# Scan matrices read back as rows from DRAM, and another order of the state-space items: a two-layer hybrid trunk on one core

## The reference, cut to what matters

```
dt = exp(log_dt);  a = exp(lambda * dt)              # complex, one per group g and state p
b_bar = ((a - 1) / lambda) * b                       # 64 groups, 64 states, 16 inputs
x[l,g,p] = sum_h u[l,g,h] * b_bar[g,p,h]
h[l] = a * h[l-1] + x[l]                             # over 256 tokens
y = Re(sum_p c[g,h,p] * h[l,g,p]) + d * u            # then gelu, a GLU gate, silu(z)
```

## Time and profile before

| what | value |
|---|---|
| median of 3 runs | 952.5 us (952.48 to 952.61) |
| the profiled execution | 952.75 us, of it 951.0 us span |
| PE busy | 936.0 us, 98% of the span |
| DVE busy | 610.0 us, 64% |
| ACT busy | 575.4 us, 60% |
| POOL busy | 111.3 us, 12% |
| chain that ended last | PE 82%, ACT 7%, DVE 6%, issue 3% |
| HBM | 173 GB/s over the span |

### The profile page before, as it was taken

The page is one execution under the profiler, slowest core; times in us unless marked ns, Lnnn a source line. Parts: engine busy times, 40 slices in busy tenths (PEclk is TensorE's granted clock), DMA queues, the critical chain, the costliest instruction groups (busy, mean ns, idle before and its releaser), DMA issues.

```text
span 951.0 us, 15769 instructions
## 1 busy us (share of the span) xinstructions
PE 936.0 (98%) x5939; PEld 796.3 (84%) x5939; DVE 610.0 (64%) x971; ACT 575.4 (60%) x928; POOL 111.3 (12%) x126
## 2 busy tenths in 40 slices
PE   7999999999999999999999999999999999999998
PEld 7998888778878999888888788888888888888886
DVE  4688889799797954855644555555555555555553
ACT  4689886876967746544545573555456545554332
POOL 3101002011020000000002540220021002200000
PEclk9999999999999999999999999999999999999999
DMA  8776544445343467555999986668999866654662
GB/s 285 185 190 196 156 133 134 136 135 175 112 140 127 137 198 266 179 192 190 175 166 180 195 239 169 182 174 160 171 160 172 197 175 178 176 175 156 212 213 85
DMA packets 116007, 165.83 MB, mean 174 GB/s; under 512 B 19301, under 2 KB 56298, under 8 KB 115690
## 3 DMA queue, kind: packets, MB, share of 16 engines
q1 hardware_dynamic: 99504, 159.67, 64.0%
q10 hardware_dynamic: 16442, 5.33, 2.3%
HBM read 162.86 MB, written 2.11 MB: 173 GB/s over the span
## 4 chain that ended last, share of the span: by engine, by line
PE 82%; ACT 7%; DVE 6%; issue 3%; DMA 1%; POOL 1%; ACTq 0%; SPq 0%; DVEq 0%
PE bank L456 21%; PE bank L458 21%; PE bank L457 21%; PE bank L483 3%; PE bank L484 3%; PE bank L485 3%; ACT wh L969 2%; ACT res L1078 2%; PE bank L600 1%; ACT res L1090 1%; DVE wl L977 1%; ACT scr L1230 1%; DVE scr L1747 1%; PE bank L592 1%; DMA res<-in_x 1%
## 5 line engine op out<-in xcount | busy, mean ns | idle before, releaser
L977 DVE TENSOR_TENSOR wl<-raw,wh 128x1024 fp32r<-128x1024 f32 x295 | 362.0, 1231 | 252.7 <-ACT wh L969 251.5
L969 ACT ACTIVATE wh<-raw 128x1024 fp32r<-128x1024 f32 x295 | 310.5, 1058 | 190.2 <-PE bank L458 119.5
L456 PE MATMUL bank<-wh,xh 128*128 128x512 f32 x768 | 307.1, 400 | 0.3 <-DVE wl L977 0.3
L458 PE MATMUL bank<-wh,xl 128*128 128x512 f32 x768 | 300.0, 391 | 0.0
L457 PE MATMUL bank<-wl,xh 128*128 128x512 f32 x768 | 299.2, 390 | 0.0
L458 PEld LDWEIGHTS bank<-wh,xl 128*128 128x128 f32 x768 | 144.1, 188 | 31.1
L456 PEld LDWEIGHTS bank<-wh,xh 128*128 128x128 f32 x768 | 144.3, 188 | 29.0 <-DVE wl L977 0.7
L457 PEld LDWEIGHTS bank<-wl,xh 128*128 128x128 f32 x768 | 144.5, 188 | 27.7
L456 PE MATMUL bank<-wh,yh 128*128 128x512 f32 x256 | 100.5, 393 | 0.0
L458 PE MATMUL bank<-wh,yl 128*128 128x512 f32 x256 | 99.7, 390 | 0.0
L457 PE MATMUL bank<-wl,yh 128*128 128x512 f32 x256 | 99.6, 389 | 0.0
(11 more groups left out here) (317 smaller groups left out, 1022.4 us busy)
## 6 DMA issues: line engine op xcount, KB each, us to landing
raw<-in_o_w_in SPq DMA_DIRECT2D x128, 512.0 KB
raw<-in_e_w_in SPq DMA_DIRECT2D x130, 256.0 KB, 3.3
raw<-in_e_w_out SPq DMA_DIRECT2D x32, 512.0 KB
raw<-in_o_w_out SPq DMA_DIRECT2D x32, 512.0 KB
raw<-in_e_w_in SPq DMA_DIRECT2D x31, 512.0 KB
raw<-in_s_w_glu SPq DMA_DIRECT2D x8, 512.0 KB
res<-in_x SPq DMA_DIRECT2D x8, 256.0 KB, 6.8
res<-in_x SPq DMA_DIRECT2D x1, 2048.0 KB, 9.6
```

The costliest lines, as they stand in the source:

```text
L456: nc.tensor.matmul(o, l_hi, w_hi, start=first, stop=False)
L458: mm = nc.tensor.matmul(o, l_lo, w_hi, start=False, stop=last)
L969: nc.scalar.activation(wh[:, j % RING, :], raw[:, j % RING, :], ACT.Copy).then_inc(hi_done, 1)
L977: nc.vector.tensor_tensor(wl[:, j % RING, :], raw[:, j % RING, :], wh[:, j % RING, :].bitcast(F32), ALU.subtract).then_inc(lo_done, 1)
```

## The change

The 16 transposes for each item go. Instead B and the powers 1 to 4 of a are turned once, in step 0: `p_rows_turn` (2 transposes, after slot 1) and `b_rows_turn` (4 transposes each, after slots 2 and 3); ACT copies them out (`rows_out_of`, slots 2 to 4), SP stores them to DRAM (`rows_keep`, 20 DMAs of 256-byte pieces in two parts, at its units 12 and 13) and loads them for each item spread over 128 partitions (`rows_load`, four calls of three DMAs; for item 0 behind units 14, 14, 15, 15, later behind units 6 to 9). DVE multiplies them (`s5_rows`, two calls of three operations of 128 x 512, slots -4 and -3), and ACT spreads the product into `xin` (`s5_spread`, slots -3 and -2, two activations each). `s5_powers` goes. The state is taken one token further, so that `s5_far` needs three powers where it had five, and `cc`'s first part and the new `b0` are copies by ACT (`s5_own`, slot -6). `s5_hold` goes from one DVE operation to eight activations. `s5_near` no longer waits for `xin`. `angles` moves to slots -2 and -1, `table` with it to slot 0; the second call of `s5_far` to slot -5; `s5_low` of all items to the z chunks; `b_blocks` from slot 3 to slot 0 of step 0. On PE `s5` now always stands ahead of `attention` in a slot.

```diff
-TAB_SLOT, FAR_SLOT, BA_SLOT = [0, 0], [-7, -4], [-10, -4]
-T_SLOT = [-2, -1, -1, -1]
-NEAR_SLOT, HOLD_SLOT, SKIP_SLOT = [-1, 2], -3, -8
+TAB_SLOT, FAR_SLOT, BA_SLOT = [-2, -1], [-7, -5], [-4, -3]
+SPREAD_SLOT = [-3, -2]
+KEEP_UNIT, LOAD_UNIT, LOAD_FIRST = (12, 13), (6, 7, 8, 9), (14, 14, 15, 15)
+NEAR_SLOT, HOLD_SLOT, SKIP_SLOT, OWN_SLOT = [-1, 2], -3, -8, -6
+LOW_SLOT = {10: 0, 11: 1, 13: 2, 15: 3}
...
+            def rows_keep(part):
+                sp.wait_ge(bp_sb, 3)
+                for k in range(2 * part, 2 * part + 2):
+                    sp.dma_start(p_rows[k, :, :, :, :].rearrange("g r i n -> i (g r) n"),
+                                 st_p[GP * k:GP * (k + 1), :, :, :].rearrange("p g r n -> p (g r) n")).then_inc(bp_out, 16)
+                for k in range(4 * part, 4 * part + 4):
+                    for g in range(2):
+                        sp.dma_start(b_rows[g, :, :, k:GP:TB, :].rearrange("h f b n -> h (f b) n"),
+                                     st_b[16 * k:16 * (k + 1), :, :, g, :].rearrange("p f b n -> p (f b) n")).then_inc(bp_out, 16)
+            def rows_load(i, k):
+                sp.wait_ge(xin_sb, 2 * i) if i else sp.wait_ge(bp_out, 16 * 20)
+                tiles = slice(TB * i, TB * i + TB)
+                for g in range(2):
+                    at = slice(32 * k + 16 * g, 32 * k + 16 * g + 16)
+                    src = p_rows[k, g, :, tiles, :].rearrange("r i n -> r (i n)")
+                    sp.dma_start(p_of[at, :, :], src.rearrange("(o r) n -> o r n", o=1).to_broadcast([16, 2, TB * 64]))\
+                        .then_inc(bt_in, 16)
+                sp.dma_start(b_t[32 * k:32 * k + 32, :, :],
+                             b_rows[:, :, :, tiles, :].rearrange("g h f i n -> (g h) f (i n)")).then_inc(bt_in, 16)
...
-            def s5_turn(i, k):
+            def p_rows_turn():
+                pe.wait_ge(pw_done, 1)
+            def b_rows_turn(half):
+                pe.wait_ge(bc_b, 1)
...
             def s5_near(i, h):
-                pe.wait_ge(xin_sb, 4 * i + (3 + h))
                 if h == 0:
+                    if i:
+                        pe.wait_ge(gelu_done, i)
                     pe.wait_ge(cc_done, 2 * i + 2)
+                    pe.wait_ge(b0_done, i + 1)
                     pe.wait_ge(dd_done, i + 1)
...
+            def s5_spread(i, r):
+                act.wait_ge(made_done, 2 * i + (r + 1))
+                for g in range(2):
+                    ins = nc.scalar.activation(xin[:, :, r, 64 * g:64 * g + 64], made[r].rearrange("p (i n) -> p i n", i=TB),
+                                               ACT.Copy, scale=of_group[:, g:g + 1])
+            def s5_hold(i):     
+                for t in range(TB):
+                    ins = nc.scalar.activation(mg[:, t, :], later, ACT.Copy, scale=mag_all[:, TB * i + t:TB * i + t + 1])
...
                     at = s5_at(n, s, i)
                     if TAB_SLOT[1] + 1 == at:
                         table(i)
-                    for k in range(4):
-                        if T_SLOT[k] + 1 == at:
-                            s5_turned(i, k)
+                    if OWN_SLOT == at:
+                        s5_own(i)
+                    if HOLD_SLOT == at:
+                        s5_hold(i)
+                    for r in range(2):
+                        if SPREAD_SLOT[r] == at:
+                            s5_spread(i, r)
                     for h in range(2):
                         if PAD_SLOT[h] == at:
                             s5_pad(i, h)
...
+            def s5_rows(i, r):
+                if r == 0:
+                    dve.wait_ge(bt_in, 16 * 12 * (i + 1))
+                v.tensor_tensor(first, pr, (br, bi)[r], ALU.mult)
+                link(v.tensor_tensor(second, pi, (bi, br)[r], ALU.mult))
+                v.tensor_tensor(made[r], first, second, ALU.add if r else ALU.subtract).then_inc(made_done, 1)
...
-                     (1, 6): b_factors, (1, 7): powers, (2, 2): lam_end, (2, 3): b_blocks}
+                     (1, 6): b_factors, (1, 7): powers, (2, 0): b_blocks, (2, 2): lam_end}
```

More of the change, by code:

```diff
@@ L389, in chunk, with rows_aside @@
                     load(c, j, src)
+                    if CH_DA <= c < CH_Z:
+                        rows_aside(*divmod(UNITS * (c - CH_DA) + j, 2 * UNITS))
+            def rows_keep(part):
[17 more added lines that the diff above has]
+                             b_rows[:, :, :, tiles, :].rearrange("g h f i n -> (g h) f (i n)")).then_inc(bt_in, 16)
+            def rows_aside(i, s):
+                for k in range(HOP):
+                    if i == 0 and k < 2 and KEEP_UNIT[k] == s:
+                        rows_keep(k)
+                    if (LOAD_UNIT if i else LOAD_FIRST)[k] == s:
+                        rows_load(i, k)
             w_e, w_eo, w_o, w_oo, w_g = d["e_w_in"][0], d["e_w_out"][0], d["o_w_in"][0], d["o_w_out"][0], d["s5_w_glu"][0]
@@ L646, in fox_late, with s5_near @@
                     fox_p_turn(i, at_pt[s])
-            def s5_turn(i, k):
-                if k == 0:
-                    pe.wait_ge(ba_done, i + 1)
-                    pe.wait_ge(bc_c, 4)
+            def p_rows_turn():
+                pe.wait_ge(pw_done, 1)
+                for r in range(2):
+                    mm = nc.tensor.transpose(scb[:, r * P:(r + 1) * P], pw[:, r, 1:HOP + 1, :].rearrange("p k i -> p (k i)"), ident)
+                mm.then_inc(bp_ps, 1)
+            def b_rows_turn(half):
+                pe.wait_ge(bc_b, 1)
+                for b in range(2):
+                    for r in range(2):
+                        at = (2 * r + b) * P
+                        mm = nc.tensor.transpose((xb, yb)[half][:, at:at + P], bc_all[:, 2 * half + b, r, :], ident)
+                mm.then_inc(bp_ps, 1)
+            def s5_near(i, h):
+                if h == 0:
                     if i:
                         pe.wait_ge(gelu_done, i)
-                elif k == 1:
+                    pe.wait_ge(cc_done, 2 * i + 2)
+                    pe.wait_ge(b0_done, i + 1)
+                    pe.wait_ge(dd_done, i + 1)
+                else:
                     pe.wait_ge(qkt_sb, head_no(i, 1) + 1)
@@ L726, in s5_out_y @@
                     mm.then_inc(y_ps, 1)
[L728 to L732, removed]
             def beside(n, s, heads):
[L735 to L738, removed]
+                s5(n, s)
                 for a, at in heads:
                     attention(a, at)
-                if turns:
-                    s5(n, s)
             def s5(n, s):
@@ L796, in c_turn @@
                     pe.wait_ge(rbc_done, 1)
+                else:
+                    pe.wait_ge(bp_sb, k)
                 for e in range(CT // 2):
@@ L835, in step @@
                         beside(i, s, ([] if first else [(i - 1, s)]) + [(i, s - 2 * UNITS)])
+                        if first and s == 1:
+                            p_rows_turn()
+                        if first and 2 <= s < 4:
+                            b_rows_turn(s - 2)
                         if first and 3 <= s < UNITS - 1:
@@ new lines, in s5_rows @@
+            def s5_rows(i, r):
+                (pr, pi), (br, bi) = ([x[:, k, :] for k in range(2)] for x in (p_of, b_t))
+                if r == 0:
+                    dve.wait_ge(bt_in, 16 * 12 * (i + 1))
+                    first, second = prod[0].rearrange("p r n -> p (r n)"), prod[1].rearrange("p r n -> p (r n)")
+                else:
+                    first, second = pr, pi
+                v.tensor_tensor(first, pr, (br, bi)[r], ALU.mult)
+                link(v.tensor_tensor(second, pi, (bi, br)[r], ALU.mult))
+                v.tensor_tensor(made[r], first, second, ALU.add if r else ALU.subtract).then_inc(made_done, 1)
@@ L1769, in s5 @@
                         if BA_SLOT[part] == at:
-                            s5_powers(i, part)
+                            s5_rows(i, part)
                     if at == SKIP_SLOT:
                         s5_skip(i)
-                    if at == HOLD_SLOT:
-                        s5_hold(i)
                     for h in range(2):
@@ L1779, in s5 @@
                             rotate_out(i, h)
-                    if HIGH_SLOT + 1 == at:
-                        s5_low(i)
+                if n == DA_PAIRS and s in LOW_SLOT:
+                    s5_low(LOW_SLOT[s])
             def log_steps():
```

139 lines of the change are left out of this document (67 added, 72 removed).

## The result

The changed kernel took 982.16 us (median of 4 runs, 980.14 to 983.75) beside 952.49 us of the kernel before: 1.0314 times as long, with a 95% interval of 1.0289 to 1.034. The sign was as forecast, and most of the places; the time lies outside the range of 955 to 975. The profiled execution has a span of 981.7 us, 30.7 more than before. Two executions of the whole record lie far off the others (1163.24 us of the kernel before, 2134.88 us of the run with angles and table in their old slots) and are in no median here.

A forecast was written before the change was run, and what follows sets the result against it. PE, busy nearly the whole span, was taken to bound the kernel. Step 0 +4.5, item 0 +3.7, items 1 to 3 +6.0 and `y_turn` -2.7 gave +11.5 us, so 964.0, range 955 to 975.

The forecast's parts named there:

- Turns gone: On PE around slot -2 to slot 0, each item loses 2.20 us of turns.
- `y_turn`'s wait gone: In the steps, PE no longer waits for DVE's `head_out`: -2.7 us.
- hand-over at T + 12.9: `s5_in_x` starts 12.9 us after PE ends its slot -2 unit (T), 2.0 later than before; items 1 to 3: +6.0.
- T + 8.4: PE alone would reach `s5_in_x` 8.40 us after ending its unit of slot -2 (T), if nobody else is late.
- the clock: Rival, 25%: PE's clock falls in the new waits of the four items, four falls, 6.8 us more, 970.8.
- my terms gave 3.3: From the first `s5_in_x` to `x1_turn`, the changed kernel was forecast 3.3 us longer.
- SP's queue: Rival, 8%: issues of 128 pieces take 0.8 us rather than 0.46, so item 0 waits 11 us longer: 975.
- +3.7 forecast: Item 0's `s5_in_x` at T + 14.6: 3.0 us wait for SP's rows, 1.3 saved on the table load.
- The 2 us for the landing of the last store: In item 0's SP chain, time assumed for the last store to land, which no row shows: 2 us.
- PE's slack of three units: For stream weights, PE's slack takes up what SP's queue adds to a stream load.
- Step 0: +4.5 forecast: `b_blocks` ahead of the remainder makes PE's slot 3 unit 4.1 us late; four turns add 0.4.
- Everything behind `x1_turn` at nothing: The rest of the kernel after the first turn behind the GLU was forecast to change by 0.

The follow-up runs named there:

- the filled waits: Changed kernel with 18 unneeded matmuls of 128 columns ahead of `s5_in_x` in each item: 971.86 us, ratio 1.021.
- the kernel with three stores: Changed kernel with the rows laid out in DRAM so that 3 DMAs store them instead of 20, 16 loads per item instead of 12: 971.66 us.
- the three mended: Changed kernel with table in slot 1, `b_blocks` halved behind the remainders of slots 0 and 1 of step 0, and 3 store DMAs: 944.19 us.
- half filling: Changed kernel with 9 unneeded matmuls ahead of `s5_in_x` in each item, instead of 18: 975.95 us, ratio 1.0255.
- `b_blocks` moved: Changed kernel with `b_blocks` in halves behind the remainders of slots 0 and 1 of step 0, PE's turns later: 977.81 us.

## Why the prediction was wrong

- **Turns gone, `y_turn`'s wait gone, hand-over at T + 12.9.** Right: 12.55 measured, angles at T + 5.4 for 5.7, PE 4.1 us before that at its own pace (T + 8.4, as forecast). Without the clock the stretch from the first `s5_in_x` to `x1_turn` is 2.4 us longer than before (292.73 - 290.31); my terms gave 3.3.
- **The step that failed: the clock.** The sum took every matmul at the upper level, at no cost behind a wait, and priced the fall as a rival with 25% and 4 falls of 1.7 us, 6.8. It came, and larger: six falls and not four, at 2.0 us on average. In the items it cost 8.0 us (shown by the filled waits). In slot 3 of step 0 the unit took 4.45 us, and 2.87 with the same wait and no fall in the kernel with three stores: 1.6. Behind item 0's late remainder it took 5.42 for 2.9: 2.5. Sum 12.1 us. The last two terms compare executions; no run fills those waits. My price came from 18 matmuls of 256 columns at the start, each 0.09 late; ahead of the z chunks a low stretch holds 7 to 11 matmuls of 512 columns, each 0.20 late, and for items 1 and 2 `s5_in_x` as well. The Trainium skill (TensorE: Matmul & The Clock Gate, "Why this matters for your kernels") has it that gaps of idling between bursts bring the lower level back; the trace agrees, four of four waits of 4.0 to 4.2 us did (PEclk 0.94, 0.90, 0.90 and 0.94 in the 30 us behind them). It should have been the forecast, since the only rows on it spoke for it and nothing against. The prediction also weighed the clock and SP's queue as alternatives, each inside its range when it comes alone. Both came, and SP's late rows brought one of the falls that were not counted.
- **Item 0: +3.7 forecast, +9.5 measured**, of it 2.5 the clock. SP's stores of B took 0.65 to 0.71 us each instead of 0.46, so DVE waited 6.2 us instead of 3.0. (The 2 us for the landing of the last store held: the stores of B landed a median of 2.2 us after their issue.) The sum let only `near` be late by DVE's wait, and took PE's slack of three units as enough for the stream. But the remainder stands behind that wait in DVE's list, and PE waited 4.83 us for it. The rival on SP's queue had the right mechanism; its 0.8 us and 11 us were too large here.
- **Step 0: +4.5 forecast**, 6.8 measured from the first unit of step 0 to slot 7, 1.6 of it the clock and 0.7 more of waits and turns. Another 0.5 us stands ahead of step 0; that unit started between 60.0 and 61.8 us in all runs, so this says nothing of the change.
- **Everything behind `x1_turn` at nothing**: +3.5 us in the profiled execution. PE's instructions are the same in both kernels from there on, and nearly all of the 3.5 us stands in two of its waits, here of the changed kernel and then the one of the kernel before that answers to the second:

```profile
550.49 0.50 PE L501 MATMUL bank<-wh,xh 128*128 128x512 f32 x1 [1.53 <-DVE wl L1016]
...
561.30 0.65 PE L637 MATMUL bank<-con,uz 128*128 128x128 f32 x4 [2.32 <-POOL uz L2194]
```
```profile
530.59 0.66 PE L592 MATMUL bank<-con,uz 128*128 128x128 f32 x4 [0.63 <-POOL uz L2131]
```

Both go back to ACT. It stores `decay_rows` to DRAM and then waits in its own list for the landing, before it may load them again (460 to 700 us; of the changed kernel, then of the one before):

```profile
ACT wh L1008 <- DMA decay_rows<-scr: 8.2, 1, 8.2
```
```profile
ACT wh L969 <- DMA decay_rows<-scr: 4.6, 1, 4.6
```

The same store landed 9.2 us after its issue, and 5.6 before the change. In the other four kernels with 20 stores that are read here it took 7.3 to 7.5 us, in the seven with 3 stores or none 5.2 to 5.7; the part behind `x1_turn` took 546.6 to 548.3 us with 20 stores and 544.2 to 545.5 without. So it goes with the stores. Why a store should land later some 440 us behind them no run shows, and no experiment aimed at it; it stays open.

The excess over the forecast, 19.2 us of the profiled spans, is then 12.1 clock, 3.3 rows of item 0, 1.2 step 0 and start, 3.5 the end, less 0.9 in the items.

## What to carry to other kernels

In this kernel a wait of some 4 us on an otherwise dense matrix engine cost 5.4 to 6.9 us: the wait itself and 1.3 to 2.8 us of matmuls at the low level behind it. Price these from the start. If the wait can't be removed, filling it with matmuls that nobody needs gives the second part back. A change that removes work from the engine that bounds the kernel pays only if the engines that hand work to it come no later than before: here some 10 us of gain were in the edit all along, and three placements hid them; with the three mended 8.5 us showed, with 4.0 us of waiting left in item 0. DMAs of a shared in-order queue are to be counted one by one, and merged by choosing the layout in DRAM before their slot is tuned.

## What the runs showed of the hardware that I had not expected

- Over all runs whose profiles are read here, every one of PE's 26 waits from 3.8 to 6.7 us after the start had the low level behind it. Waits of 1.2 us never did before the change. In between it is not the wait's length alone: the clock fell behind waits of 2.01 and 2.65 us (half filling) and of 2.42 us (table back in slot 1, at 533.98 us), and not behind 2.02 us (half filling) or 2.68 us (full filling, at 551.27 us).
- The same wait didn't have the same price. In item 3, behind a wait of 4.0 us, the first call of `s5_in_x` to the second took 13.47 us in the changed kernel and 14.93 with `b_blocks` moved, against 12.17 in the filled one: 1.3 and 2.8 us.
- SP needs more time for a store of 16 partitions in 64-element pieces (0.65 to 0.71 us, a mean of 0.80 for one group of eight with `b_blocks` moved) than for one of 128 partitions in the same pieces (0.47 to 0.51), although that moves eight times as much.
